# Order of the norm chains inside the last output products, token halves for the first four feature blocks, and a table load in pieces

## The reference

```
layer "even": norm+modulate -> projections (qB,kB,vB,pA) -> recurrence + window attention -> w_out -> gated residual
              norm+modulate -> square(relu(u @ w_ff1)) @ w_ff2 -> gated residual            (512 tokens)
layer "odd" : norm+modulate -> projections (qD,kD,vD,vC,qC,kC) -> global and neighbourhood attention
              -> w_out -> gated residual -> norm -> ff1, ff2 -> gated residual              (256 tokens from w_out on)
second block: norm -> projections (qN, kcv, ...) -> attention, retention -> merge
              norm -> w_ffn_up, conv, gate -> w_ffn_down -> final norm                      (256 tokens)
rms_norm(x, g) = x * rsqrt(mean(x*x) + eps) * g ;  neighbourhood attention adds a bias table gathered from c_rpb
```

## Time and profile before

| | before |
|---|---|
| runs, us | 2075.05, 2072.39, 2075.25 (median 2075.05) |
| profiled execution, us | 2072.41 |
| its span, us | 2070.6 |
| PE, DVE, ACT, POOL busy | 90%, 53%, 43%, 10% |
| mean granted clock of PE | 0.954 |

### The profile page before, as it was taken

How to read it: one execution, slowest core, us unless ns; L and a number is a source line. 1 busy time by engine, 2 the same in 40 slices (tenths; PEclk the granted TensorE clock), 3 DMA queues, 4 the chain that set the end, 5 groups by cost and what they waited for, 6 DMA issues and landing times.

```text
span 2070.6 us, 40061 instructions
## 1 busy us (share of the span) xinstructions
PE 1859.6 (90%) x16962; PEld 1554.9 (75%) x16962; DVE 1097.0 (53%) x1671; ACT 892.2 (43%) x1430; POOL 214.7 (10%) x214
## 2 busy tenths in 40 slices
PE   5899879889888999999997799799978998779997
PEld 3777558778777788888886676798876676569985
DVE  1457565465545554324335666565445674556863
ACT  2326555344332353214325256565342465346652
POOL 0000034525253000000000100010000000000210
PEclk9999889999999999999998899999999999789999
DMA  8232233222231312332223320355545434134552
GB/s 271 93 122 89 91 112 104 84 84 84 84 104 64 117 51 98 102 102 88 95 91 61 124 81 25 119 184 183 196 121 164 139 103 157 62 122 163 184 160 105
DMA packets 201376, 237.18 MB, mean 115 GB/s; under 512 B 14347, under 2 KB 158573, under 8 KB 201197
## 3 DMA queue, kind: packets, MB, share of 16 engines
q1 hardware_dynamic: 195856, 227.33, 34.6%
q10 hardware_dynamic: 5341, 7.30, 1.0%
HBM read 233.56 MB, written 1.05 MB: 113 GB/s over the span
## 4 chain that ended last, share of the span: by engine, by line
PE 77%; DVE 9%; ACT 5%; POOL 2%; SPq 2%; issue 2%; DMA 2%; ACTq 0%; DVEq 0%; POOLq 0%
PE bank L1381 18%; PE bank L1383 17%; PE bank L1382 17%; PE bank L1573 9%; ACT window L2442 2%; SPq L2899 2%; DVE window L1875 2%; PE bank L1561 2%; PE bank L1540 2%; PE bank L1552 2%; PE bank L1432 1%; PE bank L1446 1%; PE bank L1758 1%; PE bank L1580 1%; PE bank L1544 1%
## 5 line engine op out<-in xcount | busy, mean ns | idle before, releaser
L1381 PE MATMUL bank<-window 128*128 128x512 f32 (+1 forms) x2136 | 761.0, 356 | 56.6 <-DVE window L1924 28.8
L1382 PE MATMUL bank<-window 128*128 128x512 f32 (+1 forms) x2136 | 748.0, 350 | 0.0
L1383 PE MATMUL bank<-window 128*128 128x512 f32 (+1 forms) x2136 | 747.9, 350 | 0.0
L1875 DVE TENSOR_TENSOR window<-arena,window 128x2048 fp32r<-128x2048 f32 (+1 forms) x164 | 372.1, 2269 | 273.5 <-ACT window L2442 271.7
L1381 PEld LDWEIGHTS bank<-window 128*128 128x128 f32 x2136 | 414.1, 194 | 120.9 <-DVE window L1924 30.0
L2442 ACT ACTIVATE window<-arena 128x2048 fp32r<-128x2048 f32 (+3 forms) x292 | 377.1, 1291 | 209.8 <-PE bank L1383 121.7
L1383 PEld LDWEIGHTS bank<-window 128*128 128x128 f32 x2136 | 413.3, 193 | 50.9
L1382 PEld LDWEIGHTS bank<-window 128*128 128x128 f32 x2136 | 414.5, 194 | 48.7 <-issue 0.2
L2442 ACT ACTIVATE arena<-bank 128x256 f32<-128x256 f32 (+1 forms) x298 | 127.3, 427 | 368.6 <-PE bank L1383 130.1
L1573 PE MATMUL bank<-arena 64*64 64x64 f32 (+1 forms) x5888 | 215.9, 228 | 18.6 <-DVE arena L1367 10.2
L1573 PEld LDWEIGHTS bank<-arena 64*64 64x64 f32 x5888 | 202.5, 138 | 35.1 <-DVE arena L1367 11.9
(11 more groups left out here) (285 smaller groups left out, 1670.3 us busy)
## 6 DMA issues: line engine op xcount, KB each, us to landing
arena<-in_w_ff SPq DMA_DIRECT2D x64, 1024.0 KB, 5.4
arena<-in_w_ada SPq DMA_DIRECT2D x48, 1024.0 KB, 5.4
arena<-in_w_in SPq DMA_DIRECT2D x23, 1024.0 KB, 5.0
arena<-in_w_ffn_up SPq DMA_DIRECT2D x22, 1024.0 KB, 5.1
arena<-in_w_ffn_down SPq DMA_DIRECT2D x10, 1024.0 KB, 5.1
arena<-in_w_in_even SPq DMA_DIRECT2D x9, 1024.0 KB, 5.5
arena<-in_w_out SPq DMA_DIRECT2D x8, 1024.0 KB, 5.0
arena<-in_w_in_odd SPq DMA_DIRECT2D x8, 1024.0 KB, 6.9
```

The lines of the kernel that those rows point to most:

```text
L1381: e.matmul(o, rr(l[0]), rr(r[0]), start=start, stop=False)
L1382: e.matmul(o, rr(l[0]), rr(r[1]), start=False, stop=False)
L1383: return e.matmul(o, rr(l[1]), rr(r[0]), start=False, stop=stop)
L1875: e.tensor_tensor(rr(raw), raw, rr(w.high, F32), SUB).then_inc(*ve.tick(w.ready))
```

## The change

In `out_proj` the last two chunks of c = 1 (y = len-2 and len-1) are multiplied together, tile by tile: first chunk len-2 for the tile, then chunk len-1. Between the two stands the "x" step of the tile two before, behind the second its "x hi" and "x lo". Behind the out block of a tile come its residual, square and diag at once; behind the last tile these alternate with the x, hi and lo of the tile before it. The same pairing of chunks holds where there are no chains (`then` empty).

`fm_first` takes four feature blocks from two chunks and a number of tokens n; it does all four blocks for the first n/2 tokens, then all four for the second half. It is used for qB and ff1 of layer 0 (n = 512) and now also for qN, ff1 of layer 1 and up (n = 256, halves of 128 tokens, each waiting for one tile). Both chunks are loaded ahead of it.

The 32 bias DMAs are issued four at a time, behind each of the eight vC steps.

```diff
 def out_proj(...):
             for y, (W, k0, x0, nk) in enumerate(parts):
                 cols(("out", name, c, y), W, c * 512, 512, k0, nk)
-                if c == 1 and y == len(parts) - 1:
+                if c == 0 or y < len(parts) - 2:
+                    step("out", name, c, y, tuple(range(ntok)))
+                elif y == len(parts) - 1:
                     for m in range(ntok):
+                        step("out", name, c, y - 1, (m,))
+                        if then and m > 1:
+                            next(then[m - 2])
                         step("out", name, c, y, (m,))
+                        if then and m > 1:
+                            next(then[m - 2])
+                            next(then[m - 2])
                         step("out block", name, c, m)
                         give("out", name, c, m)
                         if then:
-                            going.append(then[m])
-                            going = advance(going)
-                else:
-                    step("out", name, c, y, tuple(range(ntok)))
+                            last = then[m - 1] if m == ntok - 1 else iter(())
+                            next(last, None)
+                            for _ in range(3):
+                                next(then[m])
+                                next(last, None)
...
-        while going:
-            going = advance(going)
+        run(*then[-2:])
...
-    step("load bias")
+    bias_loads = iter(range(0, len(bias_pairs), 4))
 def c_proj():
...
                 step("vC", y, k)
                 if y:
                     give("vC", k)
+                step("load bias", next(bias_loads))
                 yield
...
-        def fm_first(w, x, us, points):
+        def fm_first(ws, x, us, points, n=512):
             for h in range(2):
-                s = slice(256 * h, 256 * h + 256)
+                s, m = slice(n // 2 * h, n // 2 * (h + 1)), len(points) // 2
                 for f, u in enumerate(us):
-                    pe.wait_ge(w.ready, u.before, *points[2 * h:2 * h + 2])
+                    w, f0 = ws[f // 2], f % 2 * 128
+                    pe.wait_ge(w.ready, u.before, *points[m * h:m * h + m])
                     for k in range(8):
-                        i = split_product(u.b[:, s], [a[:, k, f * 128:f * 128 + 128] for a in (w.v.hi, w.v.lo)],
+                        i = split_product(u.b[:, s], [a[:, k, f0:f0 + 128] for a in (w.v.hi, w.v.lo)],
                                           [a[:, k, s] for a in (x.hi, x.lo)], k == 0, k == 7)
...
-        def qN_(j):
-            fm(chunks["qN", j // 2], (j % 2) * 128, X, N256, bank("qN", j), *second_x, last=j % 2)
+        def qN_first():
+            fm_first([chunks["qN", j] for j in range(2)], X, [bank("qN", j) for j in range(4)], second_x, 256)
...
+        def up_first():
+            fm_first([chunks["up", j] for j in range(2)], X, [bank("up", j) for j in range(4)], up_x, 256)
...
-        def load_bias():
+        def load_bias(n):
             sp.wait_ge(*stage("ff0"))
-            load(landed_bias, at("bias"), bias_pairs)
+            load(landed_bias, at("bias"), bias_pairs[n:n + 4])
```

More of the change, by code:

```diff
@@ L452, in out_proj @@
         outs[name] = Out(parts, x, ntok, O, points, ready, add, gate, then)
-        going = []
         for c in range(2):
@@ L532, in program @@
     even_x = xr
+    for j in range(2):
+        cols(("qB", j), W_e, 1920 + j * 256, 256)
     for j in range(4):
[L535 to L542, removed]
+        take("qB", j)
+    step("qB first")
+    for j in range(4):
         step("qB", j)
@@ L938, in ffn @@
             for j in range(nt):
[L939 to L943, removed]
+                first = part == 0 and j < 4
+                if j % 2 == 0 and not (first and j):
+                    for y in (0, 1) if first else (j // 2,):
+                        cols(("ff1", i, part, y), I["w_ff1"][i], (part * nt + 2 * y) * 128, 256)
+                if first and j == 0:
+                    for f in range(4):
+                        take("ff1", i, 0, f)
                     step("ff1 first", i)
-                if not (n == 512 and part == 0 and j < 2):
+                if not first:
                     take("ff1", i, part, j)
@@ L1119, in program @@
     second_x = xr
+    for j in range(2):
+        cols(("qN", j), W_2, j * 256, 256)
     for j in range(4):
-        if j % 2 == 0:
-            cols(("qN", j // 2), W_2, j * 128, 256)
         take("qN", j)
+    step("qN first")
+    for j in range(4):
         step("qN", j)
@@ L1312, in program @@
     for j in range(44):
-        if j % 2 == 0:
-            cols(("up", j // 2), W_u, j * 128, 256)
-        take("up", j)
+        if j % 2 == 0 and j != 2:
+            for y in (0, 1) if j == 0 else (j // 2,):
+                cols(("up", y), W_u, y * 256, 256)
+        if j == 0:
+            for f in range(4):
+                take("up", f)
+            step("up first")
+        if j > 3:
+            take("up", j)
         step("up", j)
@@ L1399, in tm @@
             i.then_inc(*pe.tick(u.full, *([w.used] if last else [])))
-        def fm_first(w, x, us, points):
+        def fm_first(ws, x, us, points, n=512):
             for h in range(2):
-                s = slice(256 * h, 256 * h + 256)
+                s, m = slice(n // 2 * h, n // 2 * (h + 1)), len(points) // 2
                 for f, u in enumerate(us):
-                    pe.wait_ge(w.ready, u.before, *points[2 * h:2 * h + 2])
+                    w, f0 = ws[f // 2], f % 2 * 128
+                    pe.wait_ge(w.ready, u.before, *points[m * h:m * h + m])
                     for k in range(8):
-                        i = split_product(u.b[:, s], [a[:, k, f * 128:f * 128 + 128] for a in (w.v.hi, w.v.lo)],
+                        i = split_product(u.b[:, s], [a[:, k, f0:f0 + 128] for a in (w.v.hi, w.v.lo)],
                                           [a[:, k, s] for a in (x.hi, x.lo)], k == 0, k == 7)
                     if h:
-                        i.then_inc(*pe.tick(u.full, *([w.used] if f else [])))
+                        i.then_inc(*pe.tick(u.full, *([w.used] if f % 2 else [])))
         N256, N512 = slice(0, 256), slice(0, 512)
@@ L1488, in qB_first @@
         def qB_first():
[L1489 to L1493, removed]
+            fm_first([chunks["qB", j] for j in range(2)], X, [bank("qB", j) for j in range(4)], even_x)
         def kB_():
@@ L1700, in ff1_first @@
         def ff1_first(i):
-            fm_first(chunks["ff1", i, 0, 0], X, [bank("ff1", i, 0, 0), bank("ff1", i, 0, 1)], ffs[i].xr)
+            fm_first([chunks["ff1", i, 0, y] for y in range(2)], X, [bank("ff1", i, 0, j) for j in range(4)], ffs[i].xr, ffs[i].n)
         def ff1(i, part, j):
             F = ffs[i]
-            if not (F.n == 512 and part == 0 and j < 2):
-                fm(chunks["ff1", i, part, j // 2], (j % 2) * 128, X, slice(0, F.n), bank("ff1", i, part, j),
-                   *(F.xr if part == 0 else ()), last=j % 2)
+            if part or j > 3:
+                fm(chunks["ff1", i, part, j // 2], (j % 2) * 128, X, slice(0, F.n), bank("ff1", i, part, j), last=j % 2)
         def qD_(j):
@@ L1827, in mix2 @@
                  last=m == 1)
+        def up_first():
+            fm_first([chunks["up", j] for j in range(2)], X, [bank("up", j) for j in range(4)], up_x, 256)
         def up(j):
-            fm(chunks["up", j // 2], (j % 2) * 128, X, N256, bank("up", j), *(up_x if j == 0 else ()), last=j % 2)
+            if j > 3:
+                fm(chunks["up", j // 2], (j % 2) * 128, X, N256, bank("up", j), last=j % 2)
         steps = {"vc 0": lambda: vc(0), "vc 1": lambda: vc(1), "mod": mod, "turn": turn, "x": norm_x, "spread": spread, "out": out,
-                 "qB first": qB_first, "qB": qB_, "kB": kB_, "vB": vB_, "sink": sink, "pA": pA_, "rotate": rotate_, "swap": swap_,
+                 "qB first": qB_first, "kB": kB_, "vB": vB_, "sink": sink, "pA": pA_, "rotate": rotate_, "swap": swap_,
                  "scores": scores, "turn p": turn_p, "values": values, "unit grams": unit_grams, "unit turned": unit_turned,
@@ L1838, in tensor @@
                  "ff1 first": ff1_first, "ff1": ff1, "qD": qD_, "kD": kD_, "vD": vD_, "qC": qC_, "kC": kC_, "vC": vC_,
-                 "d sums": d_sums, "qN": qN_, "kv": kv_, "vsw": vsw_, "gt": gt_, "compress": compress, "turn hid": turn_hid,
+                 "d sums": d_sums, "qN first": qN_first, "kv": kv_, "vsw": vsw_, "gt": gt_, "compress": compress, "turn hid": turn_hid,
                  "compressed": compressed, "qkr": qkr, "vg": vg, "ret s": ret_s, "ret o": ret_o, "branch": branch_,
-                 "ret turn": ret_turn, "z turn": z_turn_, "mix2": mix2, "up": up,
+                 "ret turn": ret_turn, "z turn": z_turn_, "mix2": mix2, "up first": up_first, "up": up,
                  "end": lambda name: pe.mark(at("stage", name, pe))}
```

## The result

The changed kernel takes 2149.24 us (median of 4 runs, 2148.59 to 2154.12) against 2073.72 for the kernel before, run beside it (2069.0 to 2075.25): a ratio of 1.0373, 95% interval 1.035 to 1.0397. The forecast was 2101, range 2070 to 2126: the direction is right, the time is not. The profiled execution's span is 2146.8 instead of 2070.6, so 76.2 us have to be found.

What follows compares the result with a forecast made beforehand. PE was taken to bound the kernel, busy nine tenths of the span, the rest waits behind norms. A to F, 2.9 + 4.9 - 12.9 + 9.4 + 11.6 + 10.0, gave +25.9 us: median 2101, range 2070 to 2126.

Steps and rivals of the forecast that it cites:

- D: mix1 and ff1 of layer 1: +9.4 us, with a late second chunk and then 144 products at 0.116.
- E: ff2 of layer 1 and qN: +11.6 us, second chunk no earlier and 144 products left instead of 48.
- F: up: +10.0 us, start earlier by one tile's lo but 192 products at 0.116 plus 2.6 at half clock.
- Columns bind: Rival at the 128-column sites: a product costs 0.06 us, so not slower, 2073.5; 0.18 together with the skill's 81 ns.
- two passes: Rival at the 128-column sites: a product takes two matmuls, 0.22 us, giving +80, 2155; chance 0.13.
- rival 2: At the 128-column sites: each product costs 0.22 us as two passes, +80, 2155; chance 0.13.
- A: qB: +2.9 us, from a 2.3 us wait ahead of the third block and 0.6 for more halves.
- B: mix0 and ff1 of layer 0: +4.9 us, from a wait inside mix0, a later last diagonal and costlier halves.
- C: ff2 of layer 0 and odd layer: -12.9 us, qD starting as now and vC no longer waiting behind bias issues.
- The spread saves nothing: Rival at vC: the second vC chunk, behind 16 bias issues, stalls as long as the first did; +12.9, 2114; chance 0.08.

Runs made afterwards that it cites:

- e6: Kernel before with only out_proj's paced norm chains, no four-block order, halves or spread loads: 2088.89 us, ratio 1.0076.
- e3: Kernel before with blocks 8 to 23 of up, mid-stretch without waits, computed in halves of 128 columns: 2114.32 us, ratio 1.0207.
- e4: Kernel before with only the 32 bias loads spread over the eight vC products: 2064.82 us, ratio 0.9955.
- e5: Kernel before with blocks 0 to 15 of up, right behind the wait for X, in halves of 128 columns: 2184.68 us, ratio 1.0546.
- e2: Changed kernel with each block at ff1 of layer 1, qN and up computed twice over all 256 columns: 2115.1 us, ratio 1.0205.

## Why the prediction was wrong

**The step that failed** is the time at half clock in D, E and F. The prediction added "192 x 0.116 = 22.3 plus 2.6 for half clock until 1865" at up, and 1.2 and nothing at qN and ff1: it took over from the earlier trace rows that the clock is back some 7 us behind a wait, and there the products that follow the wait have 256 columns. With 128 it doesn't come back before the halves end. At up the 192 products take 192 x 0.213 = 41 instead of 24.9; at ff1 and qN 144 x 0.213 = 30.7 instead of 16.7 and 17.9. That is 16 + 14 + 13 = 43 of the 50.5 us by which D, E and F came out above the prediction. Of the other 7.5, 4.3 is a later start at D: the second chunk's first product is at 1328.03, or 1329.1 without the -1.1 carried there, against 1324.8. The chain ahead of it was mis-sized: the last x step starts at 1316.70, or 1317.8 without what was carried there, where the prediction had the diagonal at 1314.6. e6 shows what pacing does there by itself, 8.3. At E the second chunk's wait is 8.70, against 6 to 7.

**The price of a 128-column product was right for the clock at which its rows were read.** At the full clock it is 0.111 in e3, against 0.116, between the load's 0.11 and the block's 0.12. *Columns bind* (0.06) and *two passes* (0.22 at any clock) are both excluded by e3. The time of rival 2, 2155, is close to the result by luck, because half clock nearly doubles the price too; its mechanism is wrong. The Trainium skill ("TensorE: Matmul & The Clock Gate", Back-to-back issue gap) gives about 81 ns for 128 columns in a stream with weight loads; these runs show 111 ns at the full clock.

**A is right:** a wait of 2.19 ahead of the third block (2.3 predicted), +3.0 in all. **B has its steps right:** 2.82 inside mix0 (2.8) and 8.06 ahead of the last diagonal (some 8); the sum was 2.7 short: the last diagonal came at 740.2, or 738.6 without the 1.6 carried there, against 736.8, and the wait for ff1's second chunk was 2.00, costed at 0.6. **C is right in its mechanism:** the paced chains cost ff2 a wait of 9.95, qD is no earlier, and vC follows vD with 0.75 instead of 6.21 and 4.96 of waiting. Its -12.9 is -10.3, a difference no larger than what untouched stretches move. What e4 shows of it: the mask came 12.1 us later, some 8 without the 4.3 carried there, not some 3, and what it stretched was not a split with room, as the prediction had it, but D's normalisation, on PE's path. *The spread saves nothing* falls with e4. The rows of the kernel before that these readings rest on, POOL's mask and the transposes behind vD:

```profile
1142.71 9.10 POOL L2867 TENSOR_TENSOR arena<-arena 128x2048 f32<-128x2048 f32 x2 [474.01 <-DMA arena<-in_c_rpb]
...
1147.94 1.11 PE L1501 MATMUL bank<-arena 128*128 128x128 f32 x4 [6.21 <-ACT arena L2442]
```

## What to carry to other kernels

A block split along the moving columns to start it early can cost nearly the whole block a second time: a 128-column product cost 0.111 here, a 256-column one 0.120. Price it by a row of a narrow product, not by its columns. Above all, look at which clock the split products will begin with: behind a wait they began at half clock here and stayed there for as long as they lasted, so a wait of 5 us, shortened by 1.4, came to 26. And an instruction moved off one critical operation is to be followed to what it lies beside next, as the mask was here, three times.

## What the runs showed of the hardware

The clock's return hung here on what PE ran and not only on its having no gap: 768 products of 128 columns back to back stayed at 0.50 for 164 us (e5), with PE busy in every stretch, while 256-column products at up, also behind a wait of 5.35 (e2, twice per block), were at 1.00 five us behind their start. The Trainium skill ("TensorE: Matmul & The Clock Gate", What's actually happening) says that "activity releases the throttle"; in e5 164 us of products that left PE no idle time by the profile did not release it. Matmuls of 128 columns in full float32 were followed by the full clock: at ff1 of layer 1 it was back by 1320, where the x step that begins at 1316.70 ends (first row of the stretches), and again by 1361, behind the 16 that begin at 1358.81.

At half clock 128 and 256 columns both cost 0.213 (medians of neighbouring starts in the changed kernel), at the full clock 0.111 and 0.120, so at both the smaller product is bound by something that doesn't shrink with its columns; that it is the weight load fits but was not separated by a run of its own. Why the halves hold the full clock but don't regain it stays open.
